# Latent attention: the low halves of eight weight blocks, made on GpSimd in place of VectorE

## The reference

```
q        = (rmsnorm(q_lat)  @ w_q_b)     # per head: 128 columns and 64 rotary ones
k_nope,v = (rmsnorm(kv_lat) @ w_kv_b)    # per head: 128 + 128 columns
p        = softmax(concat(q_nope, q_rope) . concat(k_nope, k_rope) * 192 ** -0.5)
o        = p @ v
```

## Time and profile before

| what | value |
|---|---|
| median of 3 runs | 2833.24 us (2833.1 to 2835.24) |
| the profiled execution's own time | 2835.0 us |
| its span, first to last instruction | 2833.4 us |
| mean granted TensorE clock | 0.997 |
| instructions | 42083 |
| busy: TensorE, VectorE, ScalarE, GpSimd | 98%, 66%, 36%, 7% of the span |

### The profile page before, as it was taken

One profiled execution on the slowest core, in us unless ns is written; L12 is line 12 of the kernel. 1 busy time (PEld: TensorE's weight loads), 2 busy tenths in 40 slices (PEclk: granted clock), 3 DMA queues, 4 the chain that ended last, 5 costly groups with the idle time before them and its releaser, 6 DMA issues.

```text
span 2833.4 us, 42083 instructions
## 1 busy us (share of the span) xinstructions
PE 2784.9 (98%) x15881; PEld 2483.3 (88%) x15881; DVE 1880.5 (66%) x2917; ACT 1032.9 (36%) x1804; POOL 186.9 (7%) x260
## 2 busy tenths in 40 slices
PE   8999999999999999999999999999999999999997
PEld 2689999878888778999999999999999888888886
DVE  8766666586995888866666666666666455424338
ACT  7522333234554114544444444444444312112121
POOL 0131111000001000000000000000000000000005
PEclk9999999999999999999999999999999999999999
DMA  9764334362334745222222222222222545224232
GB/s 391 281 196 152 125 130 135 124 199 69 110 118 168 250 156 201 86 104 88 103 103 98 103 92 99 102 88 103 103 98 95 202 127 172 75 92 139 75 117 92
DMA packets 105545, 379.84 MB, mean 134 GB/s; under 512 B 13934, under 2 KB 14226, under 8 KB 103530
## 3 DMA queue, kind: packets, MB, share of 16 engines
q1 hardware_dynamic: 89664, 321.56, 32.8%
q0 software_dynamic: 15488, 56.95, 5.7%
q10 hardware_dynamic: 298, 0.04, 0.0%
HBM read 346.97 MB, written 33.48 MB: 134 GB/s over the span
## 4 chain that ended last, share of the span: by engine, by line
PE 89%; DVE 5%; DMA 4%; ACT 1%; issue 1%; SPq 0%; ACTq 0%; POOLq 0%; DVEq 0%
PE ps L2158 15%; PE ps L2160 15%; PE ps L2159 15%; PE ps L2708 12%; PE ps L2710 12%; PE ps L2709 12%; DMA mraw<-in_wstream 2%; PE ps L2361 1%; PE ps L2326 1%; DMA fst<-fscr 1%; DMA raw<-in_wstream 1%; DVE ps L2086 1%; PE ps L2635 1%; PE ps L2636 1%; PE ps L2637 1%
## 5 line engine op out<-in xcount | busy, mean ns | idle before, releaser
L2708 PE MATMUL ps<-actl,ringh 128*128 128x320 f32 x1344 | 415.4, 309 | 0.2 <-DVE ringl L1933 0.2
L2709 PE MATMUL ps<-acth,ringh 128*128 128x320 f32 x1344 | 415.3, 309 | 0.0
L2710 PE MATMUL ps<-actl,ringl 128*128 128x320 f32 x1344 | 415.3, 309 | 0.0
L2158 PE MATMUL ps<-dwh,fring 128*128 128x512 f32 x820 | 319.4, 390 | 1.3 <-DVE dwl L2061 1.3
L2160 PE MATMUL ps<-dwh,fring 128*128 128x512 f32 x820 | 319.2, 389 | 0.0
L2159 PE MATMUL ps<-dwl,fring 128*128 128x512 f32 x820 | 319.1, 389 | 0.0
L2708 PE MATMUL ps<-acth,ringh 128*128 128x320 f32 x1008 | 311.5, 309 | 0.0
L2709 PE MATMUL ps<-actl,ringh 128*128 128x320 f32 x1008 | 311.5, 309 | 0.0
L2710 PE MATMUL ps<-acth,ringl 128*128 128x320 f32 x1008 | 311.5, 309 | 0.0
L2061 DVE TENSOR_TENSOR dwl<-raw,dwh 128x1024 fp32r<-128x1024 f32 x82 | 100.4, 1224 | 288.9 <-ACT dwh L1439 288.9
L1933 DVE TENSOR_TENSOR ringl<-raw,ringh 128x512 fp32r<-128x512 f32 x252 | 173.6, 690 | 156.5 <-ACT ringh L1350 156.5
(11 more groups left out here) (364 smaller groups left out, 5913.3 us busy)
## 6 DMA issues: line engine op xcount, KB each, us to landing
raw<-in_wstream SPq DMA_DIRECT2D x503, 512.0 KB, 3.7
mraw<-in_wstream SPq DMA_DIRECT2D x64, 512.0 KB, 7.7
fscr<-fst POOLq DMA_DIRECT2D x44, 320.0 KB, 2.4
fst<-fscr SPq DMA_DIRECT2D x21, 640.0 KB, 4.4
acc<-in_xT SPq DMA_DIRECT2D x8, 640.0 KB, 16.0
oscr<-ost POOLq DMA_DIRECT2D x16, 320.0 KB, 3.5
ostage<-oscr POOLq DMA_DIRECT2D x16, 320.0 KB, 4.0
acc<-in_xtok POOLq DMA_DIRECT2D x4, 1280.0 KB, 8.3
```

The costliest lines, as they stand in the source:

```text
L2158: mm(out, ah, bh, start=first, stop=False)
L2708: mm(out, ringh[:, s, w], ah, start=first, stop=False, skip_group_check=True)
L2709: mm(out, ringh[:, s, w], al, start=False, stop=False, skip_group_check=True)
L2710: ins = mm(out, ringl[:, s, w], ah, start=False, stop=last, skip_group_check=True)
```

## The change

GpSimd's loop gets, behind the copy of the values of head a, the subtract for block `B_HEAD + a + 2`; it waits until all blocks ahead of it in the order are done with and until ScalarE has made the high half. VectorE's split in the loop goes. Where VectorE would next raise `lo_ready`, at the start of the next pass and ahead of the output projection, it gets a wait until GpSimd has raised it, so that the count keeps its order.

```diff
@@ GpSimd, loop over heads
                 pool.wait_ge(pv_ready, NH + a)
                 v_of_head(a, vm)
 
+                n = B_HEAD + a + 2
+                pool.wait_ge(lo_ready, POS[("w", n)])
+                pool.wait_ge(hi_ready, n + 1)
+                nc.gpsimd.tensor_tensor(lo_of(n), raw[:, slot_of("w", n), :], hi_of(n).bitcast(f32),
+                                        ALU.subtract).then_inc(lo_ready, 1)
+
@@ VectorE, loop over heads
                 if h < NH:
                     if h:
+                        dve.wait_ge(lo_ready, POS[("w", B_HEAD + h + 1)] + 1)
                         gemv(None, 72 + 3 * h)
...
                         if s == 0:
                             low(4, ql_[:, HT:T], ps[3][:, 0:HT], qh[:, HT:T])
                             gemv(None, 74 + 3 * h)
-                        if s == 1:
-                            split(None, B_HEAD + h + 2)
@@ VectorE, ahead of the output projection
+            dve.wait_ge(lo_ready, POS[("w", B_HEAD + NH + 1)] + 1)
             for b in range(32):
```

## The result

The changed kernel takes 2865.5 us in the median of four runs (2864.5 to 2870.3), the kernel before 2833.9 in the median of four: ratio 1.0117, 95% interval 1.0105 to 1.0128. It is slower, as forecast, by 31.6 us in place of 24.4, and 0.5 us above the upper end of the range. The profiled execution is the longest of the four: 2870.3 us, span 2868.6.

The account below looks back on a forecast made before the run. TensorE, busy 98% of the span, was taken as the bound, its attention waits being for `pb`. Holds 16.7 plus clock falls 7.7 made 24.4 us; on the profiled 2835.0, less 1.8 to the median: 2857.6 us, range 2847 to 2865.

Parts of the forecast that it names:

- The freed time on VectorE is worth nothing: Eight 1.22 us splits leave VectorE: at most 0.04 us a pass, taken as nothing; rival with 2827.4 us had chance 0.04.
- 2.35 us for a subtract: Each of eight 128x1024 subtracts added on GpSimd takes 2.35 us; upper end 2.74 us, also covering fp32r output.
- The hold reaches TensorE whole: GpSimd's subtract holds VectorE's chain before the late transposes: 2.18 us in passes 1 to 7, 1.47 in pass 0, 16.7 total.
- The race that I set at 0.04 us between GpSimd and L1623: Behind the value copy, GpSimd's subtract starts at 803.59, ahead of L1623 at 803.63, and so holds it.
- the rival in which GpSimd loses it: L1623 and L1626 pass before or beside the subtract: price 0 to 1.5 us, 2833 to 2835 us; chance 0.10.
- New waits, the later `lo_ready`, the loads of `ostage`: VectorE's added waits, the count 4 us later and the loads behind the last subtract stay hidden and cost nothing.
- The clock, the step that failed: Idle gaps of 2.6 us a pass halve TensorE's clock afterwards; five falls taken, 7.7 us, range 0 to 10.8.
- The clock holds: Rival: TensorE's clock does not fall, only the holds count, 16.7 us, giving 2850 us; chance 0.25.
- GpSimd is dearer: Rival: fp32r output or a hold stopping other instructions makes each subtract 4 us, about 2870 us; chance 0.06.

Follow-up runs that it names:

- experiment 7: Changed kernel with GpSimd's subtract moved ahead of its pass's output DMA and value copy, and L1612 and L1623 given one tensor input: 2832.9 us, ratio 0.9998.
- experiment 5: Kernel before the change, with L1612 and L1623 written with one tensor input: 2833.1 us in 11 runs, ratio 0.9996.
- experiment 1: Kernel before, VectorE's split kept, plus an unused 128x1024 GpSimd subtract behind the value copy in each pass: 2865.5 us, ratio 1.0113.
- experiment 4: Changed kernel with unused TensorE matmuls filling its wait for `pb`, 22 in pass 0 and 16 in each other pass: 2851.7 us, ratio 1.0059.
- experiment 6: Changed kernel with GpSimd's subtract moved ahead of the output DMA and value copy of its pass: 2843.3 us, ratio 1.0033.
- experiments 3: Changed kernel with L1612 and L1623 written with one tensor input, the second number a per-lane scalar: 2849.1 us, ratio 1.0052.
- experiment 2: Kernel before, split kept, plus a GpSimd fill of 128x2750 zeros, reading nothing, behind the value copy in each pass: 2850.0 us, ratio 1.0059.

## Why the prediction was right in its direction and too low

- **The freed time on VectorE is worth nothing.** Right: experiment 7 has the move almost without its cost and ends at 2832.9 us, where the kernel before (2833.7) and experiment 5 (2833.1) do.
- **2.35 us for a subtract.** Right: 2.36 us; the fp32r output has no price of its own (the unused one in experiment 1, with fp32 output, takes 2.36 us too).
- **The hold reaches TensorE whole.** Right in size: 16.8 us of added waits against 16.7, pass 0 with 1.44 us (3.50 - 2.06) against 1.47, pass 4 with 2.32 us against 2.18. The list before has a ninth wait, 0.76 us at 872.05, that is not in the list after; the eight late transposes alone wait 17.5 us longer. The held instruction was the wrong one, and the size came out because either way the hold ends with the subtract: the prediction let L1612 out at the copy's end and held L1623. In fact L1612, waiting since the middle of the copy, was not let in between copy and subtract and stayed until the subtract's end. The race that I set at 0.04 us between GpSimd and L1623 thus never took place, and the rival in which GpSimd loses it falls.
- **New waits, the later `lo_ready`, the loads of `ostage`.** Right: VectorE's new waits and the loads behind the last subtract appear nowhere in TensorE's waits from 698 to 909 us, and the waits and the clock account for 35.0 of the 35.2 us.
- **The clock, the step that failed:** "None to seven falls are 0 to 10.8 us; a single gap of this size is shown, so I take five: 7.7 us." The mechanism was right, the term mis-sized twice over. All eight gaps of 2.46 to 3.50 us were followed by a fall, and five of the eight falls lasted 6.83 us, not 3.41, so one costs up to 6.83 x 0.44 = 3.0 us. In the profiled execution the new falls cost 18.2 us, by experiment 4 12.3 in the median, in place of 7.7. I had taken both the length of a fall and its price from the one fall that the earlier trace rows show, and made seven times that price the upper end; a bound from one example bounds nothing. (Five and seven times 1.52 us are 7.6 and 10.6, so both figures were 0.1 to 0.2 us high besides.) With 12.3 for 7.7 the forecast would have been 2862.2 us. Of the 3.3 us that then remain, 0.7 lie in the kernel before, 2833.9 us where I had 2833.2. The other 2.6 lie in the hold, 19.2 us by experiment 4 where I had 16.7. The waits in the trace of the change show 17.5 us of it, and where the rest comes from was not followed.
- **"The clock holds"** falls with the windows of the kernel after; **"GpSimd is dearer"** comes near in time (2870) by the wrong mechanism, since no subtract took 4 us.

## What to carry to other kernels

Before work is moved from VectorE to GpSimd, look in the timeline at what VectorE has to do on the critical path in the very microseconds in which GpSimd would work: a 0.15 us instruction can be held for the whole of it. Put the work where the held instruction has slack, follow what stands behind that one on every engine (experiment 6), or give the small instructions a form that isn't held (experiments 3 and 7). Where a wait of TensorE grows from 0.5 to 2.5 us, count its price and a fall of the clock behind it, and give that fall a range well over the one example at hand.

## What was not expected of the hardware

- A VectorE instruction that waits need not be let in between two GpSimd instructions that follow one another: behind the copy, with the subtract next, it was held for 2.92 us, past the end of the copy, in the change and in experiment 1 alike. With the subtract first and the copy next, in pass 0 of experiment 6, it was let in. What decides this, the runs don't show.
- What is held depends on both sides: a subtract or a copy holds an instruction with two tensor inputs (1.60 us in pass 0 and 0.59 us in the earlier trace rows, in place of 0.16), a fill doesn't (0.15 us); both subtract and fill hold the scaling of 640 elements (2.60 and 2.17 us in place of 0.55); a one-number instruction with a scalar per lane is held by neither copy nor subtract (0.20 to 0.22 us); none ran beside a fill.
- The length of a gap alone doesn't decide whether the clock falls or for how long. In experiment 2 a gap of 2.84 us in pass 0 left it at 1.00 while three of 2.05 to 2.06 us were followed by half clock; in experiment 1 one of eight gaps of 2.45 to 3.52 us left it at 1.00. What decides it, these runs don't show; filling the gaps kept it up.
